# The norm ahead of the router, closed by token on TensorE

## The reference

```python
x = layer_norm(ALPHA * x + Mixer(x), ln1_g, ln1_b)        # mean and variance over the 1024 columns
logits = x @ router                                        # 8 experts
top_vals, top_idx = lax.top_k(logits, 2)
gates = jax.nn.softmax(top_vals)
y = sum_e combine[:, e] * ((silu(x @ w_gate[e]) * (x @ w_up[e])) @ w_down[e])
x = layer_norm(ALPHA * x + y, ln2_g, ln2_b)
```

## Time and profile before

| | |
|---|---|
| median of three runs | 1477.15 us |
| the profiled execution | 1477.94 us |
| its span | 1476.1 us |
| busy: PE, DVE, ACT, POOL | 95%, 90%, 75%, 8% |
| DMA, over the span | 464.86 MB, mean 315 GB/s |
| last mixer matmul to first expert matmul | 583.5 us to 609.1 us |

### The profile page before, as it was taken

How to read it: one execution, slowest core, us unless ns; L and a number is a source line. 1 busy time by engine, 2 the same in 40 slices (tenths; PEclk the granted TensorE clock), 3 DMA queues, 4 the chain that set the end, 5 groups by cost and what they waited for, 6 DMA issues and landing times.

```text
span 1476.1 us, 39851 instructions
## 1 busy us (share of the span) xinstructions
PE 1396.1 (95%) x17532; PEld 1150.7 (78%) x17532; DVE 1334.9 (90%) x1351; ACT 1112.9 (75%) x1070; POOL 125.0 (8%) x162
## 2 busy tenths in 40 slices
PE   9999999999999999899999999999999889898786
PEld 7778888888887887788777888787886766766663
DVE  3999999555699999899999999999999999999997
ACT  4697766544478775778888878988887987888884
POOL 2411024000162002100000000000000000000001
PEclk9999999999999999999999999999999999899998
DMA  9645466556464438899999999999999999999993
GB/s 315 248 163 167 162 240 207 192 196 224 151 239 145 164 135 328 318 357 391 411 405 396 411 405 402 411 405 400 410 406 412 411 407 411 410 399 410 411 398 125
DMA packets 141349, 464.86 MB, mean 315 GB/s; under 512 B 8235, under 2 KB 10411, under 8 KB 126801
## 3 DMA queue, kind: packets, MB, share of 16 engines
q1 hardware_dynamic: 138960, 457.21, 81.2%
q0 software_dynamic: 1920, 4.55, 1.0%
q10 hardware_dynamic: 288, 0.48, 0.1%
HBM read 460.79 MB, written 2.89 MB: 314 GB/s over the span
## 4 chain that ended last, share of the span: by engine, by line
PE 55%; DVE 33%; issue 5%; DMA 5%; ACT 2%; SPq 0%; DVEq 0%; ACTq 0%
PE ps L886 17%; PE ps L887 16%; PE ps L888 16%; DVE w_lo L2419 14%; DVE w_lo L2422 6%; DVE w_lo L1841 2%; PE ps L995 2%; ACT w_hi L1750 2%; DMA x<-in_moe_w_gate 2%; DMA stage<-in_w_in 1%; DMA stage<-in_moe_w_up 1%; DVE arena L1989 1%; DVE arena L2000 1%; DVE arena L2437 1%; DVE arena L2457 1%
## 5 line engine op out<-in xcount | busy, mean ns | idle before, releaser
L886 PE MATMUL ps<-arena,w_hi 128*128 128x128 f16 (+8 forms) x4016 | 585.5, 215 | 15.9 <-issue 13.3
L888 PE MATMUL ps<-arena,w_lo 128*128 128x128 f16 (+8 forms) x4016 | 585.3, 215 | 12.9 <-issue 12.9
L887 PE MATMUL ps<-arena,w_hi 128*128 128x128 f16 (+8 forms) x4016 | 585.2, 215 | 7.1 <-issue 7.1
L888 PEld LDWEIGHTS ps<-arena,w_lo 128*128 128x128 f16 x4016 | 394.1, 99 | 26.0 <-issue 19.5
L886 PEld LDWEIGHTS ps<-arena,w_hi 128*128 128x128 f16 x4016 | 394.2, 99 | 20.8 <-issue 10.6
L887 PEld LDWEIGHTS ps<-arena,w_hi 128*128 128x128 f16 x4016 | 394.4, 99 | 18.9 <-issue 9.6
L886 PE MATMUL ps<-xhl,w_hi 128*128 128x264 f16 x1024 | 282.6, 276 | 5.4 <-ACT z L1561 2.0
L888 PE MATMUL ps<-xhl,w_lo 128*128 128x264 f16 x1024 | 282.6, 276 | 0.0
L887 PE MATMUL ps<-xhl,w_hi 128*128 128x264 f16 x1024 | 282.6, 276 | 0.0
L1841 DVE SCALAR_TENSOR_TENSOR w_lo<-stage,w_hi 128x2048 f16<-128x2048 f32 (+1 forms) x94 | 208.9, 2246 | 67.8 <-ACT w_hi L1400 67.7
L2419 DVE SCALAR_TENSOR_TENSOR w_lo<-stage,w_hi 128x2048 f16<-128x2048 f32 x92 | 208.4, 2285 | 13.0 <-ACT w_hi L1750 12.9
(11 more groups left out here) (349 smaller groups left out, 1985.5 us busy)
## 6 DMA issues: line engine op xcount, KB each, us to landing
stage<-in_moe_w_up SPq DMA_DIRECT2D x64, 1024.0 KB, 14.5
stage<-in_moe_w_down SPq DMA_DIRECT2D x48, 1024.0 KB, 14.1
stage<-in_w_in SPq DMA_DIRECT2D x43, 1024.0 KB, 5.3
stage<-in_moe_w_gate SPq DMA_DIRECT2D x34, 1024.0 KB, 9.9
mixer_only<-in_moe_w_up SPq DMA_DIRECT2D x32, 1024.0 KB, 13.7
arena<-in_moe_w_gate SPq DMA_DIRECT2D x32, 1024.0 KB, 13.6
mixer_only<-in_moe_w_gate SPq DMA_DIRECT2D x23, 1024.0 KB, 13.3
mixer_only<-in_moe_w_down SPq DMA_DIRECT2D x16, 1024.0 KB, 14.6
```

What stands on the lines that cost most here:

```text
L886: mm(out, ah, bh, start=start, stop=False, skip_group_check=True)
L887: mm(out, ah, bl, start=False, stop=False, skip_group_check=True)
L888: return mm(out, al, bh, start=False, stop=stop, skip_group_check=True)
```

## The change

Three things are done in another way.

1. The norm ahead of the router is no longer applied to the tiles. ACT writes `x` as `z` times gain, tile by tile beside the squares, while the mean is not yet known. PE makes token rows from these raw tiles (matmuls with the identity, no transposes), and logits by token, with the raw tile as the stationary operand and the router moving. Mean and deviation are kept as rows (`s_rows`: minus the mean and the deviation, each as two fp16 rows, in 97 partitions), and one more matmul per token group closes each sum: `s_rows` times gain and bias (`gb_rows`) for the token rows, `s_rows` times their products with the router (`cd_rows`) for the logits. The reciprocal deviation by token (`rs_tok`) scales the token rows when they are split, and the difference of the two top logits.
2. What this needs is set up earlier: on ACT at s = 12 gain and bias as columns (`gb_cols`), on PE after the turned states eight small matmuls with the router (`cd`), on POOL behind the eight output DMAs two loads of gain and bias, spread over 64 and 33 partitions (`gb_land`, semaphore `gb_ld`), on ACT behind `so_out` the copy to `gb_rows`, which waits for both loads, and on POOL two subtractions for the low halves.
3. The residual is no longer multiplied into `z` by POOL. The scatter of the second visit begins each bank with matmuls of the token rows with an identity scaled by 64, and DVE copies there instead of adding. The gates are divided by ALPHA and the last epsilon is scaled to match.

Besides, the low half of PRE+3 moves on DVE from ahead of the norm to behind the split of the token rows, the high halves of PRE+4 and PRE+5 on ACT behind the ranks; the 16 unused matmuls are gone; and SP waits for other things before pieces PRE+16 and PRE+17.

```diff
@@ SP, new_home
                 elif m == 11 + TWICE:
+                    sp.wait_ge(S["s_split"], 1)
+                elif m == 12 + TWICE:
                     filled(sp, "logits")
-                elif m == 12 + TWICE:
                     filled(sp, ("xtok", 2, 1))
-                    sp.wait_ge(S["z_start"], KT)
@@ POOL
-                norm(2 * l, [("mix", l, 14 + j // 4, j % 4) for j in range(KT)], l, "ln1_b")
                 if l == 1:
-
-                    pool.wait_ge(S["nz_ready"], 3 * KT)
+                    for a, b, name in ((0, 64, "ln1_g"), (64, ROWS, "ln1_b")):
+                        pool.dma_start(gb_land[a:b, :], A[name][1, :].partition_broadcast(b - a)).then_inc(S["gb_ld"], 16)
+                    G.memset(s_rows[0:ROWS, :], 0.0).then_inc(S["s_zero"], 1)
+                    pool.wait_ge(S["mg_split"], 2 * KT)
                     for what in (xtl[:, 2, :], xth[:, 2, :]):
                         G.memset(what, 0.0).then_inc(S["rows_zeroed"], 1)
-                    for j in range(KT):
-                        pool.wait_ge(S["norm_ready"], j + 1)
-                        G.tensor_scalar(z[:, j, :], x[:, j, :], WS * ALPHA, 0.0, ALU.mult, ALU.add
-                                        ).then_inc(S["z_start"], 1)
+                    pool.wait_ge(S["gb_hi"], 1)
...
+                norm(2 * l, [("mix", l, 14 + j // 4, j % 4) for j in range(KT)], l, "ln1_b")
@@ PE
+                        if l:
+                            pe.wait_ge(S["cols_ready"], 1)
...
+                            for k in range(KT):
+                                t = mm(bank(("cd",))[0:ROWS, 0:NE], gb_cols[:, k, :], w_rt[:, k, :], start=(k == 0),
+                                       stop=(k == KT - 1))
...
-            keep_busy(bank("logits_t"), NORM_IDLE - 3)
-
-            for k in range(KT):
-                pe.wait_ge(S["norm_ready"], k + 1)
-                t = mm(bank("logits_t")[0:NE, 0:T], w_rt[:, k, :], x[:, k, :], start=(k == 0), stop=(k == KT - 1))
...
+            for k in range(4):
+                pe.wait_ge(S["zg_rows"], k + 1)
+                token_rows(k)
+            stats(2, OUT)
+            pe.wait_ge(S["zg_rows"], KT)
             empty(pe, "logits")
+            lgt = bank("logits")
             for i in range(3):
                 n = P if i < 2 else NS_
...
+                for k in range(KT):
+                    mm(lgt[0:n, i * NE:(i + 1) * NE], x[:, k, i * P:i * P + n], w_rt[:, k, :], start=(i + k == 0), stop=False,
+                       skip_group_check=True)
+            for k in range(4, KT):
+                token_rows(k)
+
+
+            pe.wait_ge(S["s_split"], 1)
+            pe.wait_ge(S["cd_rows_ready"], 1)
...
+                    if first:
+                        pe.wait_ge(S["unit_ready"], 1)
+                        for i in range(3):
+                            n = P if i < 2 else NS_
+                            for k, part in enumerate((xth, xtl)):
+                                mm(ps[:, b, i * P:i * P + n], part[0:n, i, d * P:(d + 1) * P], unit_ws[0:n, 0:n],
+                                   start=(i + k == 0), stop=False, skip_group_check=True)
@@ ACT
+                            act.wait_ge(S["gb_ld"], 32)
+                            fn(gb_rows[0:ROWS, :], gb_land[0:ROWS, :], ACT.Copy, scale=row_mask[0:ROWS, 0:1]
+                               ).then_inc(S["gb_hi"], 1)
...
+                            else:
+                                fn(x[:, d, :], z[:, d, :], ACT.Copy, scale=vec_d("ln1_g", 1, d)).then_inc(S["zg_rows"], 1)
+                        if l and s == 14:
+                            act.wait_ge(S["cd_lo"], 1)
+                            top_rows(bank(("cd",)), cd_rows, NE, free_of(("cd",)))
+                if l:
+                    norm_by_token()
@@ DVE
-                if l or 0 in FOLDED:
-                    lo(b0 + LOW_LAST[0])
...
+                V.scalar_tensor_tensor(s_rows[32:33, :], bank(mean)[32:33, 0:T], -1.0, s_rows[32:33, :], ALU.mult, ALU.subtract
+                                       ).then_inc(free_of(mean), 1)
...
+                V.tensor_tensor(s_rows[96:97, :], stat[96:97, 2, :], s_rows[96:97, :], ALU.subtract).then_inc(S["s_split"], 1)
+                own.after(own.n)
+                filled(dve, "logits")
...
             for i in range(3):
                 token_lo(i, 1)
+            lo(PRE + AHEAD - 2)
             gather_lo(CAPS[0], lambda e, part, h, b: filled(e, (part, h)))
```

More of the change, by code:

```diff
@@ L195, in psum_plan @@
                 put(("so", l))
+                if l:
+                    put(("cd",))
+                    turn[0] += 3
         if l == 0:
@@ L238, in first_visit, with second_visit @@
     return isinstance(at[0], int) and at[0] == 0 and at[1] == 0
+def second_visit(at):
+    return isinstance(at[0], int) and at[0] == 0 and at[1] == 1
 def trunk_kernel(nc, A, O):
@@ L420, in trunk_kernel @@
         y_rows = carve([3, D], start=silu_at)
+        s_rows = carve([T], F16, start=silu_at)
+        cd_rows = carve([NE + 1], F16)
+        rs_tok = carve([3])
+        assert at[0] <= silu_at + D
+        gb_land = carve([D], start=silu_at + D)
+        gb_rows = carve([D], F16)
+        gb_cols = carve([KT, ROWS])
+        assert at[0] <= silu_at + 4 * D
         GAIN_HOME = 2
@@ L1182, in _ @@
+            t.then_inc(full_of("logits"), 1)
+            pe.wait_ge(S["gb_ready"], 1)
+            for h in range(2):
+                for i in range(3):
+                    n = P if i < 2 else NS_
+                    name = ("xtok", i, h)
+                    mm(bank(name)[0:n, :], s_rows[0:ROWS, i * P:i * P + n], gb_rows[0:ROWS, h * 512:(h + 1) * 512],
+                       start=False, stop=True, skip_group_check=True).then_inc(full_of(name), 1)
             empty(pe, "ranks")
@@ L1424, in gain_columns, with top_rows @@
+            def top_rows(src, dst, width, done, rows=(0, 32, 64)):
+                for a in rows:
+                    t = fn(dst[a:a + 1, 0:width], src[a:a + 1, 0:width], ACT.Copy)
+                t.then_inc(done, 1)
             def gain_columns(q, g, b):
@@ L1646, in _ @@
                             fn(brh[:, j, :], conv_sq[:, j, :], ACT.Copy).then_inc(S["br_hi"], 1)
+                    if s == 12 and l:
+                        for a, b, name in ((0, 64, "ln1_g"), (64, ROWS, "ln1_b")):
+                            t = fn(gb_cols[:, :, a:b], vec_all(name, 1).to_broadcast([P, KT, b - a]), ACT.Copy)
+                        t.then_inc(S["cols_ready"], 1)
                     if s == 13:
```

201 lines of the change are left out of this document (128 added, 73 removed).

## The result

The changed kernel takes 1506.46 us (median of four runs, 1504.69 to 1508.15) against 1477.34 for the kernel before on the same chip: ratio 1.0198, 95% interval 1.018 to 1.0215. It is slower, as forecast, but by 29.1 us, not by 9.6; the time lies above the range of 1480 to 1493. The profiled execution took 1508.15 us, its span is 1506.4. I again call the end of the last square t0; P0 is the start of the first expert matmul, and D how much later it comes than before.

The account below looks back on a forecast made before the run. The weight stream bounds the visits, so a later first expert matmul delays the end equally. The load wait adds 11.9 us, the restructured norm returns 2.2: D +9.6, median 1486.7 us, range 1480 to 1493 (8 in 10).

Parts of the forecast that it names:

- Loads, ACT's copy, high halves.: Ahead of the norm: loads land at 580.0 us, ACT's copy ends at 581.1, two high halves at 585.2.
- my t0: Forecast end of the last square of `z`: 596.6 us, 11.9 us later than before the change.
- The tiles of `z` follow without a pause, since PE has long had the products.: After the low halves end at 587.6 us, DVE's `z` tiles run on at 0.49 us each.
- t0 to P0, 22.1 us forecast: Last square to first expert matmul: statistics, logits, token rows, routing, splits and cast take 22.1 us against 24.3 before.
- The clock.: PE, idle before t0, runs the first four microseconds of its 36 router matmuls at 1.2 GHz: 2 us more.
- The moved low half, 2.23 us ahead of P0.: DVE's low half of PRE+3, behind the token splits and ahead of the first cast, adds 2.23 us before the first expert matmul.
- The gap of pieces PRE+15 to PRE+17.: Weight stream runs dry, leaving three more pieces, 7.7 us, before the second visit; hidden, adding no more than D.
- Residual at nothing.: Second visit's 48 extra matmuls cost PE 2.4 us, hidden by PE's slack; counted as nothing.
- slower still, +14: Rival: loads at 581.5 us, PE at 1.2 GHz through all router work and early in the visit; 1491 us, chance 0.16.

Follow-up runs that it names:

- e2: Changed kernel with `cd`'s low half and ACT's three copies that free its bank moved ahead of ACT's wait for the loads: 1493.5 us, ratio 1.0108.
- e8: e3 plus a PSUM plan that no longer skips three banks behind `cd`: 1488.9 us, ratio 1.0077.
- e3: Changed kernel with `cd`'s bank freed early and ACT's load wait and `gb_rows` copy moved behind the squares of stage 14: 1488.4 us, ratio 1.0076.
- e11: e10 plus PE closing the logits ahead of the 12 matmuls of token rows 4 to 7: 1481.0 us, ratio 1.0025.
- e12: e11 plus DVE making the low half of PRE+3 right behind its last `z` of stage 15: 1481.6 us, ratio 1.0031.
- b1: Kernel before the change plus 48 fp16 matmuls in the second visit's scatter, overwritten so output is unchanged: 1477.8 us, ratio 1.0009.
- e14: e12 without the 48 residual matmuls in the second visit's scatter: 1480.0 us, ratio 1.002.
- e15: e12 plus ACT copying gathered columns ahead of the high halves of PRE+4 and PRE+5, and six unused PE matmuls before the gathers: 1479.2 us, ratio 1.0012.
- e10: e3 plus the PSUM plan without the skip, and POOL's two low-half subtractions moved behind its sums of squares: 1481.9 us, ratio 1.0031.

## Why the prediction was wrong

The direction and the path were right: P0 moves by 27.85 us, the issues from 612.20 to 680.84 us by 27.4 to 27.8, and the end follows, 30.2 us in the profile. D was 27.85 us where I had 9.6, 18.2 us more: 13.4 of them at t0 and 4.8 behind it. Step by step:

- **Loads, ACT's copy, high halves.** Right in kind, a little short in size: ACT's copy started 1.8 us later than forecast, and ACT was idle 12.92 us. Behind it the two low halves took 3.27 us each instead of 2.23, beside POOL's subtractions. Together that is 3.9 us on the start of `z` (591.49 against 587.6); e2 ends 2.6 us behind my t0.
- **"The tiles of `z` follow without a pause, since PE has long had the products."** This is the step that failed. PE had the products of stage 14 alone. Stage 15 waited for the bank of `cd`, which ACT frees behind the very wait that I had counted, and then took its full length after it (first matmul at 595.48, over at 608.9). e2 measures it: t0 610.0 with it, 599.2 without, 10.8 us of the 18.2 that I was short. I followed ACT's and DVE's lists and took PE's readiness from the trace of before, while the diff changed the plan of banks in two lines. Those lines had a second effect that I also missed, 4 us at t0 in e8 against e3, hidden in the changed kernel behind the load wait.
- **t0 to P0, 22.1 us forecast, 26.9 measured, 4.8 us short.** DVE could read the last logits 15.6 us after t0, not 10.2. The statistics were over 4.5 us after t0, where the sum had 0.6 for them: they started 2.6 us after it, since twelve token-row products stand ahead of them in PE's order and PE itself was late, and took 1.9 us themselves (612.63 to 614.52); the other twelve token-row products took 6.6 us, for which I had 2.8 and 2 for the clock, and their price at full clock is 3.8. The 24 logit matmuls, which no row had priced, took 4.1 us against 4.3, mostly at full clock. The rest, DVE's routing and the last piece, was 11.3 us against 11.9.
- **The clock.** I had it low after an idle time and then recovering. It was low for the gathers too, and low where PE was never idle: it fell at about 618 us, during the 8-column matmuls, behind statistics and token rows and with no pause since stage 15 began, and was back at about 624.8. The Trainium skill (TensorE: Matmul & The Clock Gate, HAM oscillation) describes a clock that falls when PE waits for data; this trace shows a fall with the engine busy on both sides of it:

```profile
616.00:617.00 1.00, 1.00 (x11) 1.00 (x11) 0.80 (x7) 0.94 (x3) 0.00 (x0) 1.00 0.64 156
...
618.00:619.00 1.00, 1.00 (x20) 0.94 (x19) 0.00 (x0) 0.98 (x2) 0.00 (x0) 0.50 1.04 426
```

- **"The moved low half, 2.23 us ahead of P0."** It did stand there, but at most 1.2 us of it showed: PE's gathers ended at 635.75 us and ACT's first copy at 635.6, the first cast behind the low half (L2413, from 636.14) at 636.8, and P0 is 636.91. Compared with e11, e12 has it gone and P0 stays, since ACT's copy ends as late there.
- **The gap of pieces PRE+15 to PRE+17.** Right that it is hidden: the fourth piece of the group was issued some 21 us after the first, with PRE+16 and PRE+17 behind it. In e12 all three are issued in time, in e11 they are not, and the medians are 1481.6 and 1481.0 us: the gap costs nothing that shows.
- **Residual at nothing.** Not shown to be nothing: 0.7 to 1.6 us by b1 and e14, with intervals that reach nothing. The medians of the variants are 0.1 to 2.9 us further above the kernel before than their P0 (e15: P0 0.5 earlier, median 2.1 above; changed: 27.85 and 29.1). But P0 is read from one execution: the profiled ones of e11 and e12 have P0 0.1 us apart and last 1478.66 and 1481.68 us. At most some of the excess is the residual; where the rest is, no run here settles. The clearest step in the profiles is at one place: between the issues that the kernel before makes at 835.15 and 863.01 us the shift grows by 1.0 to 1.3 us in the changed kernel, e3, e10 and e12, by at most 0.5 in the other variants, and not at all in e14. That is some 90 us behind the residual matmuls (767 to 781 us in the changed kernel), and e11, which has them too, shows 0.1 us; so it is not shown to be theirs.

The rival "slower still, +14" was the nearest. It had more of the clock, but the same wrong step, so it ended at 1491.

## What to carry over

Follow each changed wait through every resource that the waiting engine frees, PSUM banks among them, and not only through its instruction list; where a diff touches the allocation, list bank by bank who writes next and who must have read. A rotation of banks that is moved by one name moves all waits behind it, and a wait so far hidden can then be paid in series. Two waits of equal length hide each other: taking away either shows nothing, so try the fourth corner before an edit is called useless. And do not read a microsecond of the median from two profiles: single executions differ by more.
